# Router products in the reduced-precision format: split weights side by side as 72 stationary columns

## The reference

```python
g_prob = softmax(xt @ w_rg + b_rg)               # 4 group logits per frame
g_top, g_idx = top_k(g_prob, 1)
e_logits = (xt @ w_re + b_re).reshape(T, 4, 8)   # 32 expert logits per frame
e_top, e_loc = top_k(e_logits of the chosen group, 2)
weight = g_top * softmax(e_top)
```

## Time and profile before

| | |
|---|---|
| median of 3 runs | 4223.26 us (4206.2 to 4225.6) |
| the profiled execution's own time | 4211.02 us |
| its span, first to last instruction | 4209.0 us |
| its mean granted TensorE clock | 0.990 of full speed |
| setup, to the first strip's matmul | 0 to 61.7 us |
| block 0 (no router), blocks 1 to 7 | to about 2627.8 us |
| the last block's layer norm and router | 2627.8 to 2660.4 us |

### The profile page before, as it was taken

The page is one execution under the profiler, slowest core; times in us unless marked ns, Lnnn a source line. Parts: engine busy times, 40 slices in busy tenths (PEclk is TensorE's granted clock), DMA queues, the critical chain, the costliest instruction groups (busy, mean ns, idle before and its releaser), DMA issues. The chain is left out here.

```text
span 4209.0 us, 60644 instructions
## 1 busy us (share of the span) xinstructions
PE 4103.9 (98%) x20066; PEld 3411.4 (81%) x20067; DVE 2045.3 (49%) x3161; ACT 1423.7 (34%) x2510; POOL 740.6 (18%) x1020
## 2 busy tenths in 40 slices
PE   8999999999999999999999999599999999999997
PEld 7888888888888888888888888487888888888886
DVE  3554443443433433433433433577656566765664
ACT  2422311311311311311311311366555555655553
POOL 2000000001001000000000000234333333333333
PEclk9999999999999999999999999799999999999999
DMA  8786456455455455555555545577756466765562
GB/s 245 245 306 243 145 193 198 161 192 189 170 190 189 171 189 190 176 184 190 180 180 187 183 180 184 209 238 246 256 172 237 164 234 214 255 212 191 197 217 85
DMA packets 278468, 840.53 MB, mean 200 GB/s; under 512 B 47952, under 2 KB 99408, under 8 KB 226688
## 3 DMA queue, kind: packets, MB, share of 16 engines
q1 hardware_dynamic: 228400, 716.61, 50.0%
q0 software_dynamic: 49936, 121.90, 8.6%
HBM read 717.60 MB, written 178.45 MB: 213 GB/s over the span
## 5 line engine op out<-in xcount | busy, mean ns | idle before, releaser
L1095 PE MATMUL bank<-hT_hi,w_slot 128*128 128x512 f32 x2176 | 862.5, 396 | 8.7 <-DVE w_slot L883 7.2
L1097 PE MATMUL bank<-hT_hi,w_slot 128*128 128x512 f32 x2176 | 849.0, 390 | 0.0
L1096 PE MATMUL bank<-hT_lo,w_slot 128*128 128x512 f32 x2176 | 848.5, 390 | 0.0
L1727 PE MATMUL e_bank<-e_w_hi,e_xT_hi 128*128 128x512 f32 x1312 | 521.9, 398 | 14.2 <-DVE e_xT_lo L1653 12.2
L1729 PE MATMUL e_bank<-e_w_hi,e_xT_lo 128*128 128x512 f32 x1312 | 514.2, 392 | 0.0
L1728 PE MATMUL e_bank<-e_w_lo,e_xT_hi 128*128 128x512 f32 x1312 | 513.2, 391 | 0.0
L1658 DVE TENSOR_TENSOR e_w_lo<-e_raw,e_w_hi 128x1024 fp32r<-128x1024 f32 x384 | 443.9, 1218 | 115.4 <-ACT e_w_hi L1609 115.4
L1095 PEld LDWEIGHTS bank<-hT_hi,w_slot 128*128 128x128 f32 x2176 | 409.1, 188 | 106.6 <-issue 25.0
L1097 PEld LDWEIGHTS bank<-hT_hi,w_slot 128*128 128x128 f32 x2176 | 409.1, 188 | 87.3
L1096 PEld LDWEIGHTS bank<-hT_lo,w_slot 128*128 128x128 f32 x2176 | 409.6, 188 | 81.4
L1609 ACT ACTIVATE e_w_hi<-e_raw 128x1024 fp32r<-128x1024 f32 x376 | 366.2, 1053 | 0.0
(11 more groups left out here) (325 smaller groups left out, 6674.8 us busy)
## 6 DMA issues: line engine op xcount, KB each, us to landing
w_slot<-split_weights SPq DMA_DIRECT2D x353, 1024.0 KB, 4.8
e_raw<-in_w_exp_gate_dram SPq DMA_DIRECT2D x128, 512.0 KB
e_raw<-in_w_exp_up_dram SPq DMA_DIRECT2D x128, 512.0 KB
e_raw<-in_w_exp_down_dram SPq DMA_DIRECT2D x128, 512.0 KB
split_weights<-w_slot SPq DMA_DIRECT2D x50, 1024.0 KB, 5.7
h_rows<-h_rows SPq DMA_DIRECT2D x64, 512.0 KB, 7.6
x_rows<-in_x_dram SPq DMA_DIRECT2D x32, 512.0 KB, 5.4
raw<-in_w_in_dram SPq DMA_DIRECT2D x30, 512.0 KB, 6.9
```

What stands on the lines that cost most here:

```text
L1095: pe.matmul(out, hi, x_hi, start=first, stop=False)
L1096: pe.matmul(out, hi, x_lo, start=False, stop=False)
L1097: return pe.matmul(out, lo, x_hi, start=False, stop=last)
L1727: pe.matmul(out_p, hi, x_hi, start=first, stop=False)
```

## The change

The router's products are made in the format `float32r`. The weights are split once, in setup, into 36 high and 36 low columns that lie side by side in `w_r2`, 72 stationary columns. The transposed rows are split when they leave PSUM: ACT writes the high parts of both banks, and DVE subtracts to get the low parts of both. For each of the eight slices PE multiplies the 72 columns once with the high rows and once with the low rows, into the same accumulator of 72 partitions. The two halves of the result are added after the transposes back. The diff, with the declarations of the buffers and semaphores cut:

```diff
-        w_r = sb("router_weights", [P, KD, L])
+        w_r2 = sb("router_weights", [P, KD, 2 * L], F32R)
...
+        w_r = place([shared], "router_raw", [P, KD, L])
...
-        rowsT = place([end - 4 * D], "router_rowsT", [P, KD, P])
+        rowsT_hi = place([end - 8 * D], "router_rowsT_hi", [P, KD, P], F32R)
+        rowsT_lo = place([end - 4 * D], "router_rowsT_lo", [P, KD, P], F32R)
...  (setup, DVE, at the end of its program)
+                v.wait_ge(router_hi, 1)
+                v.tensor_tensor(w_r2[:, :, L:2 * L], w_r[:, :, :], w_r2[:, :, 0:L].bitcast(FP32), ALU.subtract)
...  (setup, ACT, behind the fifth meta strip)
+                    if n == TILES:
+                        a.wait_ge(consts_in, 16 * (7 + TAPS))
+                        a.activation(w_r2[:, :, 0:L], w_r[:, :, :], ACT.Copy).then_inc(router_hi, 1)
...  (ACT, take_rows)
-                    a.wait_ge(rt_ready, (b * TILES + i) * 2 + 1)
-                    a.activation(rowsT[:, 0:4, :], tp[0][:, :].rearrange("p (k c) -> p k c", k=4), ACT.Copy)\
-                     .then_inc(rt_act, 1)
+                    for half in range(2):
+                        a.wait_ge(rt_ready, (b * TILES + i) * 2 + half + 1)
+                        a.activation(rowsT_hi[:, 4 * half:4 * half + 4, :],
+                                     tp[half][:, :].rearrange("p (k c) -> p k c", k=4), ACT.Copy).then_inc(rt_act, 1)
...  (DVE, take_rows)
-                    v.wait_ge(rt_ready, (b * TILES + i) * 2 + 2)
-                    v.tensor_copy(rowsT[:, 4:8, :], tp[1][:, :].rearrange("p (k c) -> p k c", k=4))\
-                     .then_inc(rt_dve, 1)
+                    for half in range(2):
+                        part = slice(4 * half, 4 * half + 4)
+                        v.wait_ge(rt_act, (b * TILES + i) * 2 + half + 1)
+                        v.tensor_tensor(rowsT_lo[:, part, :], tp[half][:, :].rearrange("p (k c) -> p k c", k=4),
+                                        rowsT_hi[:, part, :].bitcast(FP32), ALU.subtract).then_inc(rt_dve, 1)
...  (DVE, take_logitsT and take_logits)
-                    v.tensor_copy(logitsT[0:L, :], quad[0][0:L, :]).then_inc(lgT_taken, 1)
+                    v.tensor_copy(logitsT[0:2 * L, :], quad[0][0:2 * L, :]).then_inc(lgT_taken, 1)
...
-                    v.tensor_tensor(tb["logits"][:, :, :],
-                                    quad[1][:, 0:TILES * L].rearrange("p (t l) -> p t l", l=L),
-                                    b_r[:, :].unsqueeze(1).to_broadcast([P, TILES, L]), ALU.add).then_inc(lg_taken, 1)
+                    both = quad[1][:, 0:TILES * 2 * L].rearrange("p (t l) -> p t l", l=2 * L)
+                    v.tensor_tensor(tb["logits"][:, :, :], both[:, :, L:2 * L],
+                                    b_r[:, :].unsqueeze(1).to_broadcast([P, TILES, L]), ALU.add).then_inc(lg_low, 1)
+                    v.wait_ge(lg_low, b)
+                    v.tensor_tensor(tb["logits"][:, :, :], both[:, :, 0:L], tb["logits"][:, :, :], ALU.add)\
+                     .then_inc(lg_taken, 1)
...  (PE, router_rows)
-                    for half, taken in ((0, rt_act), (1, rt_dve)):
+                    for half in range(2):
                         if i:
-                            pe.wait_ge(taken, b * TILES + i)
+                            pe.wait_ge(rt_dve, (b * TILES + i) * 2 - 1 + half)
...  (PE, router_product)
-                    pe.wait_ge(rt_act, b * TILES + i + 1)
-                    pe.wait_ge(rt_dve, b * TILES + i + 1)
+                    pe.wait_ge(rt_dve, (b * TILES + i) * 2 + 2)
+                    out = quad[0][0:2 * L, i * P:(i + 1) * P]
                     for k in range(KD):
-                        mm = pe.matmul(quad[0][0:L, i * P:(i + 1) * P], w_r[:, k, :], rowsT[:, k, :],
-                                       start=(k == 0), stop=(k == KD - 1))
+                        pe.matmul(out, w_r2[:, k, :], rowsT_hi[:, k, :], start=(k == 0), stop=False)
+                        mm = pe.matmul(out, w_r2[:, k, :], rowsT_lo[:, k, :], start=False, stop=(k == KD - 1))
...  (PE, router_logits)
-                        mm = pe.transpose(quad[1][:, i * L:(i + 1) * L], logitsT[0:L, i * P:(i + 1) * P],
-                                          ident[0:L, 0:L])
+                        mm = pe.transpose(quad[1][:, i * 2 * L:(i + 1) * 2 * L], logitsT[0:2 * L, i * P:(i + 1) * P],
+                                          ident[0:2 * L, 0:2 * L])
```

More of the change, by code:

```diff
@@ L345, in mixer @@
         end = shared + 4 * 2 * KD * TOK
-        rowsT = place([end - 4 * D], "router_rowsT", [P, KD, P])
-        logitsT = place([end - 4 * (D + TOK)], "router_logitsT", [P, TOK])
+        rowsT_hi = place([end - 8 * D], "router_rowsT_hi", [P, KD, P], F32R)
+        rowsT_lo = place([end - 4 * D], "router_rowsT_lo", [P, KD, P], F32R)
+        logitsT = place([end - 4 * (2 * D + TOK)], "router_logitsT", [P, TOK])
         assert attention_end <= end - 4 * HEADS * CHUNK
@@ L366, in mixer @@
             pool_step = sem1("pool_step")
+            router_hi = sem1("router_hi")
             ident_ready, dist_ready = sem1("ident_ready"), sem1("dist_ready")
@@ L592, in mixer @@
         lgT_ready, lgT_taken = sem("lgT_ready"), sem("lgT_taken")
-        lg_ready, lg_taken = sem("lg_ready"), sem("lg_taken")
+        lg_ready, lg_low, lg_taken = sem("lg_ready"), sem("lg_low"), sem("lg_taken")
         LN1_AT = {1 + i: i for i in range(TILES)}
@@ L823, in block_of_strips @@
                              .then_inc(hx_hi, 1)
-                a.sem_inc(rt_act, TILES)
+                a.sem_inc(rt_act, 2 * TILES)
                 for s in range(2):
@@ L874, in _ @@
                 v.sem_inc(hx_lo, 1)
-                for skipped in (ln_step, ln_moments, ln_normed, ln_done, rt_dve):
+                for skipped in (ln_step, ln_moments, ln_normed, ln_done):
                     v.sem_inc(skipped, TILES)
+                v.sem_inc(rt_dve, 2 * TILES)
                 v.sem_inc(lgT_taken, 1)
```

## The result

The changed kernel takes 4194.9 us (median of 9 runs, 4187.9 to 4200.1), the kernel before 4214.8 us in the same comparison (median of 9, 4205.0 to 4225.6). The ratio is 0.9947, with a 95% interval of 0.9935 to 0.9958: 22 us less, 18 to 27 (the two medians differ by 19.9). The forecast was 4204 from a base of 4223, a gain of 19 us. The time lies in the range 4192 to 4288 but near its lower end, since the base itself came out 8.5 us lower in this comparison. The ratio is just past the forecast's bound of half a per cent, and its interval reaches to both sides of it. So the measurement does not tell "faster" (given 0.22) from "within" (given 0.47); it does tell a gain from none.

The account below looks back on a forecast made before the run. PE was taken to set the loop's time alone. Products -19.4, logits transposes +0.4 and behind the loop +0.3 gave -18.7, rounded -19 us: 4211.0 to 4192 for the profiled execution, 4204 as median, range 4192 to 4288.

Parts of the forecast that it names:

- PE sets the blocks' time: Inside the loop PE alone sets the time, so what its program gains or loses there counts in full.
- The narrow matmul's price: Router product: 66 ns for each new matmul of 128 moving and 72 stationary columns, taken from the weight load.
- The rivals at 111 and 227 ns: Router product: narrow matmul costs a float32 pass (111 ns, 4227 us, chance 0.14) or the wide one (227, 4287, 0.27).
- p: Router product: price of one new narrow matmul, taken as 66 ns, bounded by 57 and 227; cancellation put at 114.
- The figure that the forecast named from the Trainium skill: Router product: about 81 ns for a load and matmul pair with 128 columns; gain then 12.7 us in all.
- The product's start and end: Around each router product: 0.30 us where weights can't load ahead, kept, with 0.03 more for the first load.
- something at the start of a product, such as a switch between formats: Rival at the router product's ends: without an unforeseen cost, up to 6 us more gained, 4198 us; chance 0.05.
- The four transposes of the logits: Router's logits on PE: moving 72 columns in place of 36 costs 0.06 us more a router, 0.4 over seven.
- ACT and DVE in the loop: Router visits in the loop: the added copy and subtractions cost nothing, covered by 3.8 us of slack.
- Setup: Weight split before the loop: costs nothing; constants land by 30, ACT has 3.24 us idle, DVE is free from 49.2.
- Behind the loop: Last router stage: 2.8 us of ACT and DVE work against cheaper products; sum 0.3 us, bounds -1 to +3.
- The sum: Whole kernel: -19.4 + 0.4 + 0.3 = -18.7, rounded -19 us, giving a median of 4204 us.

Follow-up runs that it names:

- control: Either kernel executed once more, unchanged; blocks took 2564.9 us for the kernel before and 2537.0 us for the changed kernel.
- the kernel before with one wait: Kernel before, products still float32; DVE waits for ACT's copy, so PE waits for DVE's alone ahead of the router's product; blocks 2565.5 us.

## Why the prediction was right

**PE sets the blocks' time: right.** Doubling the product lengthened the blocks by 28.3 us, where PE spends 29.0 more.

**The narrow matmul's price: right.** 66 ns was forecast from the weight load, 64.7 measured. The runs at 36, 72 and 128 columns (60, 64.7, 108 ns) show both of its bounds, and that at 72 columns they nearly meet. The rivals at 111 and 227 ns are out. One slip changed nothing in the end: gain and rest cancel near p = 108 ns (0.84 + 0.7 us over 448 matmuls is 3.4 ns), and not at 114. The figure that the forecast named from the Trainium skill ("TensorE: Matmul & The Clock Gate", section "Back-to-back issue gap", about 81 ns) does not hold here. The same page's rule for loads (section "LDWEIGHTS (loading the stationary operand)", columns over 1.2 GHz) gives 60 ns for 72 columns and 107 for 128. The trace agrees at 128 columns, with 108, and has 64.7 at 72; at the lower clock the rule does not hold, as 128 columns take 213 ns there.

**The product's start and end: this term was mis-sized.** The forecast carried the old 0.30 us over and added 0.03; it put the chance of more at 0.05, as "something at the start of a product, such as a switch between formats". Measured is 1.09 - 16 x 0.0647 = 0.05 us. So a product followed by a strip gained 0.98 us and not 0.69. Of the 28 products 21 are followed by the transposes of the next tile; such a visit took 2.90 us and takes 1.94, 0.96 less. Together the products gained 27.0 us and not 19.4. The guess at the cause was wrong as well: it is neither the format alone nor the waits. A load of 36 columns in float32 is not taken ahead of the running matmul, nor is the load behind the product; one of 72 in float32 is, and so is one of 36 in the reduced-precision format. Of the 0.98 us some 0.32 come from the width alone, as the kernel before padded to 72 columns shows, with everything else left as it was; its blocks are 8.7 us shorter. The format gives the rest: with float32 products at 72 columns the changed kernel's blocks took 2555.6 us, 18.8 more than with the new ones, close to the 19.4 of the forecast. The four transposes of the logits show the same pattern with their 36 and 72 partitions: a visit to them adds 0.31 us where it added 0.57 (and still does where the product is padded and the logits are not). Forecast was +0.06 each; it is -0.26, 1.8 us less over seven. 27.0 and 1.8 make the 28.8 that the blocks gave.

**ACT and DVE in the loop: right,** with less slack than thought, 2.4 us in the tightest of the visits and not 3.8: an operation of DVE's own stood in front of the subtractions there till 527.8. ACT's and DVE's timelines behind the same strip as in the earlier trace rows, changed kernel: the low half is done at 529.1, and the product that needs it starts at 531.48.

```profile
526.28 1.07 ACT L772 ACTIVATE router_rowsT_hi<-bank 128x512 fp32r<-128x512 f32 x2
531.68 0.60 ACT L766 ACTIVATE work<-bank 128x512 f32<-128x512 f32 x1 [4.33 <-PE bank L1112]
...
527.83 1.28 DVE L865 TENSOR_TENSOR router_rowsT_lo<-bank,router_rowsT_hi 128x512 fp32r<-128x512 f32 x2
```

**Setup: right.** ACT copies the weights at once behind its piece, without waiting for the constants, and its next piece comes at 37.55, against 37.66 in the earlier trace rows; DVE's part ends at 49.5:

```profile
34.14 0.17 ACT L525 ACTIVATE work<-bank 128x2 f32<-128x2 f32 x1 [2.63 <-PE bank L564]
34.21 0.43 ACT L534 ACTIVATE router_weights<-router_raw 128x288 fp32r<-128x288 f32 x1
37.55 0.41 ACT L529 ACTIVATE u_tail<-bank,work 128x1 f32<-128x1 f32 x2 [2.91 <-PE bank L564]
...
49.01 0.45 DVE L502 TENSOR_TENSOR router_weights<-router_raw,router_weights 128x288 fp32r<-128x288 f32 x1
```

**Behind the loop: inside its bounds, and something next to it was not foreseen.** Forecast was +0.3 us (-1 to +3), measured +1.3. All four products wait for the low rows there, 4.1, 2.2, 2.2 and 1.4 us, where it was 3.6, 0.9, 2.6 and 0.9. At the lower clock the 16 matmuls of a product stand 0.12 us apart, 2.0 us where it was 3.60. PE's timeline has the second and the third:

```profile
2616.34 0.38 PE L1130 MATMUL bank<-router_rowsT_hi,router_weights 128*72 128x128 f32 x1 [2.23 <-DVE router_rowsT_lo L865]
...
2618.32 1.93 PE L1122 MATMUL bank<-ident,h_rows 128*128 128x128 f32 x8
2622.48 0.38 PE L1130 MATMUL bank<-router_rowsT_hi,router_weights 128*72 128x128 f32 x1 [2.24 <-DVE router_rowsT_lo L865]
```

The clock was lower. Over this stage the mean granted clock is the third number from the end of each row, 0.60 after and 0.74 before (the windows view; length, then busy time and count of PE, PEld, DVE, ACT and POOL, then clock, share and rate of the transfers). The first row takes in the gap of 3 us behind the stage; without it the clock is 0.61. It stands at its 1.2 GHz level for more of the stage. First the changed kernel, then the kernel before:

```profile
2598.20:2634.10 35.90, 15.50 (x100) 13.73 (x100) 22.95 (x32) 4.78 (x8) 7.52 (x8) 0.60 0.38 147
```

```profile
2627.90:2660.40 32.50, 17.17 (x100) 13.97 (x100) 20.21 (x27) 2.39 (x4) 7.53 (x8) 0.74 0.42 162
```

The last tile gives an estimate of what the clock cost, since nothing covers PE there: its eight transposes took 0.58 us more and the four of the logits 0.31 more, 0.9 of the 1.0 us that the forecast misses. In the changed kernel's control the last product stood at the lower clock too and took 0.8 us more, and its stage is 1.0 us longer. PE's timeline, the changed kernel, then the kernel before:

```profile
2624.47 1.79 PE L1122 MATMUL bank<-ident,h_rows 128*128 128x128 f32 x8
2629.79 0.71 PE L1139 MATMUL bank<-ident,router_logitsT 72*128 72x72 f32 x4 [0.87 <-DVE router_logitsT L870]
...
2654.54 1.21 PE L1107 MATMUL bank<-ident,h_rows 128*128 128x128 f32 x8
2659.40 0.40 PE L1124 MATMUL bank<-ident,router_logitsT 36*128 36x36 f32 x4 [0.87 <-DVE router_logitsT L859]
```

The gap of 3 us stands between the last logits operation and the first of the routing stage. DVE's timeline, changed kernel:

```profile
2630.89 0.31 DVE L879 TENSOR_TENSOR logits<-bank,logits 128x144 f32<-128x144 f32 x1
2634.16 0.17 DVE L95 TENSOR_REDUCE lr_gmax<-logits 128x4 f32<-128x16 f32 x1 [2.97 <-PEq L628]
```

DVE waits for PE's sequencer, at the boundary of two stages. In the transfers view of 2628 to 2634.1 us there is a single packet, of an instruction queue, and it lies in this gap; a packet of its kind lies in the gap of the control and of the kernel before with one wait. In the kernel before, its control and its padded version no packet lies in the last 6 us ahead of the boundary.

```profile
DMA packets 1, 0.01 MB, mean 1 GB/s; under 512 B 0, under 2 KB 0, under 8 KB 0
...
q14 instruction: 1, 0.01, 0.4%
```

The gap was 0.3 us in both executions of the kernel before and in its padded version, and 3.0 to 3.7 in all executions of the changed kernel, of its variants and of the kernel before with one wait, which differs from the kernel before by the place of one wait. So it goes with the program and not with the router's work, and a late fetch of PE's instructions fits. That this is the cause is not shown; no run here shifts code alone.

**The sum: in part luck.** The forecast of 19 us agrees with the measured 22 since two of its errors point in opposite directions: 10 us too little gain in the blocks (19.0 against 28.8), 4 too little loss behind them (0.3 against 1.3 and 2.8). The stages leave 25; the distance from there to 22 lies within the scatter of the experts' stage.

## What to carry to other kernels

- Where PE sets the time, price a small matmul by the distance between starts in a full stream. Work out the moving side and the weight load separately, and take the longer: here, at full clock, 60 ns for 128 moving columns, and some 0.85 ns for each stationary column, 108 ns at 128. Where the two nearly meet, as at 72 columns, it came out a little above either (64.7).
- Look at the weight load in front of a group of matmuls too. If it does not start with the matmul before it, 0.3 us are lost at each visit here, a third of it in front of the group and the rest behind it. For a float32 operand of 36 columns, padding it to 72 brought them back without another change (0.23% of this kernel's time, with an interval of 0.09 to 0.38). Attention's products with 64 partitions show the same idle loads; nobody has padded them here.
- A gain in a loop is judged by the loop's length, not by one pair of total times, when a later stage scatters by more than the gain.

## What the runs showed of the hardware that was not expected

- A float32 weight load of 36 columns is not taken ahead of a running reduced-precision matmul; of 72 columns it is, and a reduced-precision load of 36 is (0.35 us of idle weight loading against none). The load behind such a group is held back too, by 0.2 us. The Trainium skill says that TensorE pulls weight loads ahead of matmuls in flight ("TensorE: Matmul & The Clock Gate", section "Step-by-step: what each phase is for") when row groups don't conflict or the load goes to the background buffer; it names no width. Why the width matters in float32 stays open. Column counts between 36 and 72 were not run; counted in partitions, float32 operands of 36 and 64 are held back and those of 72 and 80 are not.
- The reduced-precision format at 128 moving columns costs 60 ns, against 56.7 for a quarter of the 512-column distance: it has no large floor at 128 columns; fewer were not run.
- In the stage behind the loop, where PE waits for others, the granted clock was lower, 0.61 where it was 0.74 (0.63 and 0.73 in the controls), so that eight transposes between the products took 1.93 us (1.10 in the kernel before at the same place). The amount of PE's work does not explain it: the variants have 0.61 with 36 columns, 0.59 with 128, 0.79 with float32 at 72, 0.80 with each product made twice and 0.83 in the kernel before with one wait. What sets it there stays open; no run changed the clock by itself.
